# SBUF layout of a two-layer decoder kernel: matmul operands started at multiples of 512 bytes

## What is computed

```
u = rms_norm(h, norm_mix_g) @ w_in                       # 2048 -> 2112
y = concat(multiscale_pool(u[:, :1024]), latent_attention(u[:, 1024:]))
h = h + y @ w_out                                        # 2048 -> 2048
g = rms_norm(h, norm_ffn_g) @ w_up                       # 2048 -> 11264: gate, up
h = h + (silu(conv3(gate)) * up) @ w_down                # 5632 -> 2048
h = h + (p @ w_ple) * sigmoid(rms_norm(h, norm_ple_g) @ w_ple_gate)
```

## Time and profile before

| | us |
|---|---|
| median of 3 runs | 2258.12 |
| lowest and highest | 2257.59, 2258.47 |
| the profiled execution, device time | 2256.0 |
| its span, first to last instruction | 2254.4 |
| TensorE matmul busy | 2217.3 (98%) |
| VectorE busy | 1387.4 (62%) |
| ScalarE busy | 1046.5 (46%) |
| GpSimd busy | 66.5 (3%) |
| mean DMA rate | 180 GB/s |
| mean granted TensorE clock | 0.996 of 2.4 GHz |

### The profile page before, as it was taken

How to read it: one execution, slowest core, us unless ns; L and a number is a source line. 1 busy time by engine, 2 the same in 40 slices (tenths; PEclk the granted TensorE clock), 3 DMA queues, 4 the chain that set the end, 5 groups by cost and what they waited for, 6 DMA issues and landing times.

```text
span 2254.4 us, 31518 instructions
## 1 busy us (share of the span) xinstructions
PE 2217.3 (98%) x10594; PEld 1856.8 (82%) x10594; DVE 1387.4 (62%) x1768; ACT 1046.5 (46%) x1353; POOL 66.5 (3%) x152
## 2 busy tenths in 40 slices
PE   6999999999999999999999999999999999999997
PEld 5898888888888888888888988888888888888885
DVE  6567566565666565666466665566656566666755
ACT  4545544444444444446454554444444444444553
POOL 7000000000000000000000000000000000000000
PEclk9999999999999999999999999999999999999998
DMA  6653555556555555555556355555555655555562
GB/s 202 206 167 130 203 177 186 186 177 196 186 186 186 186 174 199 186 172 196 173 179 186 132 169 187 180 197 176 190 179 171 201 198 175 189 180 170 188 217 75
DMA packets 233597, 406.60 MB, mean 180 GB/s; under 512 B 14937, under 2 KB 50217, under 8 KB 233385
## 3 DMA queue, kind: packets, MB, share of 16 engines
q1 hardware_dynamic: 232041, 401.87, 53.8%
q0 software_dynamic: 656, 2.63, 0.3%
q10 hardware_dynamic: 816, 1.05, 0.2%
HBM read 403.42 MB, written 2.10 MB: 180 GB/s over the span
## 4 chain that ended last, share of the span: by engine, by line
PE 97%; DVE 1%; issue 1%; DMA 0%; ACT 0%; SPq 0%; DVEq 0%; ACTq 0%; POOLq 0%; POOL 0%
PE acc L1419 31%; PE acc L1421 31%; PE acc L1420 31%; PE tps L1476 3%; PE tps L1420 0%; PE tps L1421 0%; DMA raw<-in_w_in 0%; PE tps L1419 0%; DVE w_lo L1016 0%; PE tps L1669 0%; DVE h L1402 0%; ACT w_hi L618 0%; DVE xa_lo L1027 0%; DVE sg L1369 0%; DVE h L1374 0%
## 5 line engine op out<-in xcount | busy, mean ns | idle before, releaser
L1016 DVE TENSOR_TENSOR w_lo<-raw,w_hi 128x1024 fp32r<-128x1024 f32 (+1 forms) x770 | 919.2, 1224 | 506.8 <-ACT w_hi L837 355.2
L837 ACT ACTIVATE w_hi<-raw 128x1024 fp32r<-128x1024 f32 x508 | 525.9, 1059 | 512.2 <-PE acc L1421 512.2
L1419 PE MATMUL acc<-w_hi,xa_hi 128*128 128x512 f32 (+1 forms) x1792 | 690.5, 385 | 10.9 <-DVE w_lo L1016 6.1
L1421 PE MATMUL acc<-w_lo,xa_hi 128*128 128x512 f32 (+1 forms) x1792 | 687.1, 383 | 0.0
L1420 PE MATMUL acc<-w_hi,xa_lo 128*128 128x512 f32 (+1 forms) x1792 | 686.7, 383 | 0.0
L1419 PEld LDWEIGHTS acc<-w_hi,xa_hi 128*128 128x128 f32 x1792 | 337.5, 188 | 75.8 <-issue 10.4
L1421 PEld LDWEIGHTS acc<-w_lo,xa_hi 128*128 128x128 f32 x1792 | 337.1, 188 | 65.5
L1420 PEld LDWEIGHTS acc<-w_hi,xa_lo 128*128 128x128 f32 x1792 | 337.5, 188 | 64.2
L618 ACT ACTIVATE w_hi<-raw 128x1024 fp32r<-128x1024 f32 (+1 forms) x262 | 263.9, 1043 | 159.7 <-PE acc L1421 150.3
L1419 PE MATMUL acc<-w_hi,gt_hi 128*128 128x512 f32 x640 | 254.7, 398 | 0.0
L1420 PE MATMUL acc<-w_hi,gt_lo 128*128 128x512 f32 x640 | 253.1, 395 | 0.0
(11 more groups left out here) (204 smaller groups left out, 1365.4 us busy)
## 6 DMA issues: line engine op xcount, KB each, us to landing
raw<-in_w_up SPq DMA_DIRECT2D x176, 1024.0 KB, 5.1
raw<-in_w_down SPq DMA_DIRECT2D x88, 1024.0 KB, 5.0
raw<-in_w_out SPq DMA_DIRECT2D x32, 1024.0 KB, 5.1
raw<-in_w_ple_gate SPq DMA_DIRECT2D x32, 1024.0 KB, 5.1
raw<-in_w_in SPq DMA_DIRECT2D x24, 1024.0 KB, 5.4
raw<-in_w_ukv SPq DMA_DIRECT2D x8, 1024.0 KB, 5.8
raw<-in_w_in SPq DMA_DIRECT2D x8, 864.0 KB, 4.8
raw<-in_w_uq SPq DMA_DIRECT2D x6, 1024.0 KB, 5.9
```

The lines of the kernel that those rows point to most:

```text
L837: copy(w_hi[:, half_of(m), :], raw[:, c % RAW_SLOTS, (m % 2) * HALF:(m % 2 + 1) * HALF], ACT.Copy).then_inc(hi_done, 1)
L1016: dve.tensor_tensor(w_lo[:, half_of(m), 0:n], raw[:, c % RAW_SLOTS, at:at + n], w_hi[:, half_of(m), 0:n].bitcast(F32), ALU.subtract).then_ ...
L1419: pe.matmul(dst, a_hi, b_hi, start=first, stop=False)
L1421: return pe.matmul(dst, a_hi, b_lo, start=False, stop=last)
```

## The change

The order of the `sb` calls changes, and some small arrays become slices of one. `sumsq`, `sumsq_lat`, the six `rstd` arrays (now slices of `rstds`) and `band_lo` are put first, before `raw`; `krt` goes before `cos`; the four softmax arrays become slices of `soft`. No instruction is added, removed or moved on any engine: the instruction lists are the same but for addresses (the lines of the file shift by one).

```diff
+        sumsq = sb("sumsq", [P, TT, N_BLK])
+        sumsq_lat = sb("sumsq_lat", [P, 2, TT])
+        rstds = sb("rstds", [P, 6, TT])
+        rstd = {n: rstds[:, i, :] for i, n in enumerate(("mix", "q", "kv", "ffn", "ple", "final"))}
+        band_lo = sb("band_lo", [P, len(POOL_WINDOWS), 16], F32R)
         raw = sb("raw", [P, RAW_SLOTS, CHUNK])
         w_hi = sb("w_hi", [P, HALF_SLOTS, HALF], F32R)
...
         band_hi = sb("band_hi", [P, len(POOL_WINDOWS), 3 * P], F32R)
-        band_lo = sb("band_lo", [P, len(POOL_WINDOWS), 16], F32R)
+        krt = (sb("krt_hi", [P, 2, S], F32R), sb("krt_lo", [P, 2, S], F32R))
         cos = sb("cos", [P, TT, ROPE // 2])
         sin = sb("sin", [P, TT, ROPE // 2])
 
         prm_all = sb("prm_all", [P, L + 1, N_PRM])
         prm = prm_all[:, L, :]
-        krt = (sb("krt_hi", [P, 2, S], F32R), sb("krt_lo", [P, 2, S], F32R))
-        sumsq = sb("sumsq", [P, TT, N_BLK])
-        sumsq_lat = sb("sumsq_lat", [P, 2, TT])
-        rstd = {n: sb(f"rstd_{n}", [P, TT]) for n in ("mix", "q", "kv", "ffn", "ple", "final")}
...
-        mx = sb("mx", [P, 2, TT])
-        nmx = sb("nmx", [P, 2, TT])
-        psums = sb("psums", [P, 2, TT])
-        prec = sb("prec", [P, 2, TT])
+        soft = sb("soft", [P, 4, 2, TT])
+        mx, nmx, psums, prec = (soft[:, i] for i in range(4))
```

## The result

| | before | after |
|---|---|---|
| median | 2257.86 us (4 runs) | 2243.20 us (4 runs) |
| lowest to highest | 2256.82 to 2258.47 | 2241.99 to 2244.88 |
| ratio after / before | | 0.9936, 95% interval 0.9919 to 0.9953 |
| the profiled execution, device time | 2256.0 us | 2244.88 us |
| its span | 2254.4 us | 2243.3 us |

The change saves 14.7 us by the medians, 0.65%; the interval of the ratio allows 10.6 to 18.3 us. The forecast was 13.8 us saved and 2244.3 us.

The account below looks back on a forecast made before the run. TensorE's start-to-start matmul distances were taken to bound the kernel. Savings of 12.5 + 0.6 + 0.6 + 0.1 = 13.8 us from a 2258.1 us median gave 2244.3 us, 0.6% faster; the range was 2238 to 2301 us.

Parts of the forecast that it names:

- What bounds the kernel: TensorE's start-to-start distances, summed, make the time; its matmuls fill 98% of the span, and the change can only alter that distance.
- the surcharge: Time per 512-column matmul beyond its 213.3 ns of columns: 13.3 ns with `xa` stationary, 19.9 ns with `gt`; blamed on fetching operands.
- `gt` and `ppt`, 12.5 + 0.6 us: 1920 matmuls of `gt` and 96 of `ppt` each get 6.5 ns shorter, from 233.2 to 226.7 ns.
- `xa` behind `gt`, 0.6 us: The first six `xa` matmuls after `gt` no longer need to settle: 0.03 us saved at each of 20 changes.
- settling behind transposes: Matmuls settling faster after transposes, some 150 stretches of six at 4.5 ns: up to 4 us gain, counted only in the range.
- `xa` and `xb`, 0: 6672 matmuls against weights keep 226.7 ns because both operands shift by 384 bytes; bounds 88.7 us down, 43.4 us up.
- the absolute rival: The stationary operand's own start sets the cost, so remainder 0 costs nothing extra: some 2119 us, chance 0.17.
- the rival in which `xa` and `xb` fall into the dear step of `gt`: All 6672 matmuls of `xa` and `xb` cost 6.5 ns more and `gt` keeps its distance: 2301 us, chance 0.10.
- `pt` past `v` as a sign that equality counts: Three 256-column matmuls, both operands at 192, took 120 ns each, as `xb` past weights at 128; called weak.
- The quarter of a cycle per byte: Extra cost of 32 cycles at remainder 128 and 48 at 192, read as a law per byte past a multiple of 512.
- The rule on two independent ports: Skill text: TensorE reads moving operand and weights through separate ports, so no address would matter; sum 0, 2258 us.

Follow-up runs that it names:

- common64: The change with 64 bytes of padding in front of `raw`, shifting all operands alike; 2244.49 us, ratio to before 0.9942.
- before_scopes: The kernel before with only 192 bytes of padding behind `prec`, moving the scoped arrays to a distance of 256 from the weights; 2243.62 us, ratio 0.9941.
- scopes64: The change with 64 bytes of padding before the scoped arrays, putting `gt` and `ppt` back to a distance of 64; 2256.19 us, ratio 0.9999.
- x64: The change with 64 bytes of padding between `w_lo` and `xa`, shifting stationary activations against the weights; 2297.30 us, ratio to before 1.0180.

## Why the prediction was right

**What bounds the kernel.** Right. TensorE was the chain, no other engine's busy time changed by more than 1 us, and no new wait came. That the surcharge is one of fetching operands was concluded from its absence at 1.2 GHz. The absence holds at a distance of 64 too (last section); what it comes from, no run shows.

**`gt` and `ppt`, 12.5 + 0.6 us.** Right in mechanism and size: 226.8 ns where 226.7 was forecast, 389 ns drawn for both. The starts in one unit give 0.61 us less for the 96 matmuls of `gt`, 12.2 us in twenty units. The reason, the distance to the weights and not the start itself, is shown by common64, before_scopes and scopes64.

**`xa` behind `gt`, 0.6 us.** Right: 1.36 us for the six, and 0.026 us less per unit where 0.03 was forecast. A unit gained 0.62 us and not 0.65 because something else took 0.018 us back: the `xa` matmuls behind the transposes of `gate_tok` took 13.726 us for sixty instead of 13.712, and the transposes 0.004 us more. The prediction had settling behind transposes in its range alone, and as a gain.

**`xa` and `xb`, 0.** Right. Neither the absolute rival (2119 us) nor the rival in which `xa` and `xb` fall into the dear step of `gt` (2301 us) came about; a common shift left 226.7 ns. The price of that last one was real all the same: 54 us for the same matmuls and `gt` together, when the distance and not the common start is moved (x64).

**The total.** Over a whole execution the match is better than the measurement can show: 14.7 us is known to some 4 us only, and its closeness to 13.8 is in part luck. The unit time, 0.62 against 0.65 us, is the firmer test. Of the 13.5 us by which the two profiles differ from the first `gate_tok` transpose on, the terms read above and `ppt` account for 13.0; the rest was not traced.

**`pt` past `v` as a sign that equality counts.** The conclusion was right and the sign was worthless. At 256 columns equal starts are not even the cheapest: x64 ran those of `xb` past weights 2.5 ns faster at a distance of -64, and over all the distances tried they take 116.2 to 120.1 ns on the mean, so none costs there what 64 costs at 512 columns. The 120 ns that I read there could have come with either theory, and so could the argument that I drew from it against the absolute rival.

**The quarter of a cycle per byte.** A coincidence of two points. By that law x64 would have ended at about 2185 us, and it took 2297.

**The rule on two independent ports.** The Trainium skill, "TensorE: Matmul & The Clock Gate", "Step-by-step: what each phase is for", has it that loading the next weights takes nothing from the running matmul. If that were all, the distance between the two operands would not matter. The runs do not agree with it for this kernel: with the same instructions, 32 bytes between the two operands cost 6.3 ns per matmul and 54 us in all. Whether the weight load is what takes the time, no run shows.

## What to carry to other kernels

Where each float32r matmul of 512 columns has a weight load of its own, read the distance from start to start per stationary array, not the busy share; if two arrays in the same code differ by some 6 ns, compare where they start relative to the moving operand. Lay stationary and moving operands out so that their starts are equal modulo 256 bytes: distances of 0 and 256 were the cheap ones here, and a common alignment to 512 is only one way to get one. Small arrays between large ones are what breaks it, and an unused array of the missing size mends it.

## What the runs showed of the hardware that I had not expected

- The start-to-start distance of 512-column float32r matmuls depends on the relative start of the two operands in a way that is not simple; it fits a period of 256 bytes, of which one was tried: 226.7 ns at 0 and 256, 228.8 at 192, 232.1 at 128, 233.0 to 234.0 at 32, 64, 96, 160 and 224.
- At the granted clock of 1.2 GHz nothing of it is left, at equal starts and at a distance of 64 alike. The timeline of x64 gives six matmuls in 41.24 - 38.68 = 2.56 us, 427 ns each, where the same array costs 233 ns at 2.4 GHz:

```profile
38.68 0.63 PE L1420 MATMUL acc<-w_hi,xa_lo 128*128 128x512 f32 x1
...
41.24 0.63 PE L1420 MATMUL acc<-w_hi,xa_lo 128*128 128x512 f32 x1
```

- Using 64 of 128 stationary columns in one product of three made a unit 0.57 us slower (67.67 us), or 3 ns for each of its 192 matmuls that use `narrow`.
- What remains open is the mechanism, and with it the 13.3 ns that stay at the best distance and the odd place of 192. Starts off a multiple of 32 bytes were not tried.
